# Dense output products regrouped at the head of each fox and rwkv step, and the next tile's rows turned later

## The reference, cut to what matters

```
h = rms_norm(x, norm_g);  proj = h @ w_in                       # five groups of columns
ya = spatial_gating(...)                                        # 128-token chunks
yb = forgetting_attention(q, k, v, f, q_g, k_g)                 # "fox": causal softmax over all earlier tokens
yc = mlstm(...);  ym = memory_attention(...)
yd = rwkv7_time_mix(r, w_lo, k, v, a_lo, ...)                   # recurrence over tokens, 4 heads of 64
mixed = concat([y * silu(z) for y, z in branches])              # 2048 x 1280
x = x + mixed @ w_out                                           # 1280 x 1024
```

## Time and profile before

| | |
|---|---|
| median of 3 runs | 5005.95 us (4989.76 to 5011.58) |
| profiled execution | 5015.02 us, its span 5013.4 us |
| mean granted TensorE clock | 0.857 of full speed |
| PE busy | 4250.0 us, 85% of the span |
| DVE / ACT / POOL busy | 2656.4 / 1937.1 / 732.9 us |
| steps k = 2 to 15 of the fox and rwkv loop | 1380.2 to 2489.1 us |

### The profile page before, as it was taken

One profiled execution on the slowest core, in us unless ns is written; L12 is line 12 of the kernel. 1 busy time (PEld: TensorE's weight loads), 2 busy tenths in 40 slices (PEclk: granted clock), 3 DMA queues, 4 the chain that ended last, 5 costly groups with the idle time before them and its releaser, 6 DMA issues. The chain is left out here.

```text
span 5013.4 us, 66174 instructions
## 1 busy us (share of the span) xinstructions
PE 4250.0 (85%) x23522; PEld 3149.5 (63%) x23522; DVE 2656.4 (53%) x5590; ACT 1937.1 (39%) x4022; POOL 732.9 (15%) x755
## 2 busy tenths in 40 slices
PE   7997899985788899989879999977788887877589
PEld 5885777775566666666658888833344444555467
DVE  3113444444566655555411111068889888888546
ACT  3112232323333333333311101034677767767621
POOL 3111111100100000000000000022223333434500
PEclk9998999986588888989889999966578887787789
DMA  5326656664465555454352211210000001010033
GB/s 187 123 108 218 221 201 226 199 214 148 143 215 198 194 172 177 158 173 154 113 183 90 82 66 69 59 60 19 19 20 20 20 20 38 20 39 18 32 136 116
DMA packets 293737, 585.32 MB, mean 117 GB/s; under 512 B 47944, under 2 KB 80364, under 8 KB 293244
## 3 DMA queue, kind: packets, MB, share of 16 engines
q1 hardware_dynamic: 293408, 581.10, 34.1%
HBM read 453.03 MB, written 127.94 MB: 116 GB/s over the span
## 5 line engine op out<-in xcount | busy, mean ns | idle before, releaser
L3051 PE MATMUL ds_big<-ds_ikT,ds_iqT 64*128 64x512 f32 (+3 forms) x608 | 385.2, 767 | 76.3 <-ACT ds_iqT L3028 56.4
L3518 POOL TENSOR_TENSOR ds_E<-ds_bT 128x256 f32<-128x256 f32 x112 | 72.1, 643 | 2410.9 <-ACT ds_bT L3487 2232.1
L301 PE MATMUL g_acc<-g_ws_hi,g_hT_hi 128*128 128x512 f32 (+1 forms) x1024 | 386.9, 378 | 0.0
L302 PE MATMUL g_acc<-g_ws_lo,g_hT_hi 128*128 128x512 f32 (+1 forms) x1024 | 385.3, 376 | 0.0
L303 PE MATMUL g_acc<-g_ws_hi,g_hT_lo 128*128 128x512 f32 (+1 forms) x1024 | 385.2, 376 | 0.0
L529 PE MATMUL mm_big<-mm_gw_hi,mm_ghT_hi 128*128 128x512 f32 (+1 forms) x768 | 322.0, 419 | 30.9 <-PEq L134 30.9
L3107 DVE TENSOR_SCALAR_CACHE_REDUCE ds_seen<-ds_eq,ds_num 128x2048 uint16<-128x2048 uint16 (+13 forms) x224 | 331.3, 1479 | 26.3 <-issue 4.3
L531 PE MATMUL mm_big<-mm_gw_hi,mm_ghT_lo 128*128 128x512 f32 (+1 forms) x768 | 303.2, 395 | 0.0
L530 PE MATMUL mm_big<-mm_gw_lo,mm_ghT_hi 128*128 128x512 f32 (+1 forms) x768 | 302.7, 394 | 0.0
L3147 ACT ACTIVATE ds_signs<-ds_lo,ds_at 128x2048 bf16<-128x2048 uint16 (+13 forms) x224 | 291.3, 1301 | 2.1 <-issue 0.7
L328 DVE COPY g_stage<-g_acc 128x512 f32<-128x512 f32 (+1 forms) x64 | 41.5, 649 | 459.2 <-PE g_acc L303 459.2
(11 more groups left out here) (550 smaller groups left out, 10117.7 us busy)
## 6 DMA issues: line engine op xcount, KB each, us to landing
fox_ow<-halves SPq DMA_DIRECT2D x600, 256.0 KB, 3.2
mm_ghT_hi<-turned SPq DMA_DIRECT2D x96, 512.0 KB, 4.0
mm_ghT_lo<-turned SPq DMA_DIRECT2D x96, 512.0 KB, 5.1
proj<-g_stage SPq DMA_DIRECT2D x112, 256.0 KB, 2.0
proj<-mm_gstage SPq DMA_DIRECT2D x80, 256.0 KB, 5.0
mm_x<-proj SPq DMA_DIRECT2D x64, 256.0 KB, 3.7
second_raw<-in_w_in SPq DMA_DIRECT2D x56, 256.0 KB, 4.0
proj<-fp_stage SPq DMA_DIRECT2D x48, 256.0 KB, 2.0
```

What stands on the lines that cost most here:

```text
L301: pe.matmul(sums, hT.hi[:, k, tile], wt.hi[:, k, 0:width], start=(k == 0), stop=False)
L302: pe.matmul(sums, hT.hi[:, k, tile], wt.lo[:, k, 0:width], start=False, stop=False)
L3051: pe.matmul(big[:, n % 2, 0:wd], iqT[o, h // 2], b.ikT[o, x:x + wd], start=True, stop=True)\
```

## The change

The groups of `out_turn` move to 0.90, 0.925 and 0.95. In `out_product`, for steps whose first weights are there already (k > 2), eight products come together at the head (slices j = 0 and 1 whole, and of j = 2 the two that use the high weights); the rest of the first half is spread from 0.025 to 0.425 and the second half from 0.455 to 0.875, and the third product of a slice has a place of its own. The reload of a slot now stands 0.004 behind the product that frees it. Nothing is computed otherwise, and every wait is as before.

```diff
@@ out_turn
-    at = lambda g: 0.84 + 0.045 * g
+    at = lambda g: 0.9 + 0.025 * g
@@ out_product
-    at = lambda n, j: 0.005 + 0.4 * n + 0.37 * j / OUT_K
     cols = lambda n: slice(n * 512, (n + 1) * 512)
+
+    def at(n, j, a=0):
+
+        if n == 0 and j < 3 and ahead:
+            return 0.0002 * j if (j, a) != (2, 1) else 0.025
+        if n == 0 and ahead:
+            return 0.05 + 0.375 * (j - 3 + 0.4 * a) / (OUT_K - 3)
+        return 0.005 + 0.45 * n + 0.42 * (j + 0.4 * a) / OUT_K
@@ sync
-            yield at(n, j + 0.5 * a + 0.5)
+            yield at(n, j, a) + 0.004
@@ tensor
                 pe.matmul(bank, mS.hi[:, j], whi, start=(j == 0), stop=False)
                 pe.matmul(bank, mS.lo[:, j], whi, start=False, stop=False).then_inc(s.o_used, 1)
+                yield at(n, j, 1)
                 landed(pe, q + 1)
                 pe.matmul(bank, mS.hi[:, j], wlo, start=False, stop=(j == OUT_K - 1)).then_inc(s.o_used, 1)
```

## The result

| | before | after |
|---|---|---|
| median | 5008.8 us (4989.8 to 5027.6) | 5045.6 us (5030.9 to 5067.7) |
| ratio | 1 | 1.0081, 95% interval 1.0057 to 1.0105 |
| profiled execution | 5015.0 us | 5043.3 us |
| steps 2 to 15 in it | 1108.9 us | 1164.5 us |

A forecast was written before the change was run, and what follows sets the result against it. It took steps to be bound by PE's work, the clock it runs at, and an end where PE waits. End +14 and +2, clock at the end +9, clock at the head -24 gave +1 us: 5007 us, range 4985 to 5030 (overall 4962 to 5045).

The forecast's parts named there:

- clock at the head: At step starts, the slow clock ends 7.5 us earlier, at 0.25 us per us over 13 steps: 24 us gained.
- Their price, 0.25 us per us: At step heads, time taken to be saved per us less at half clock, averaged over the whole stretch.
- The end's work: From the fifth level's last PE group to the next step: 10.7 us instead of 8.2, plus 2.5 us.
- the net, 1.3: Step end's 2.5 us less 0.4 for a moved product and 0.8 for filled gaps; 14 us in 11 steps.
- Clock at the end: At step ends, the longer wait lets the clock fall earlier: 0.8 us per folded step, 9 us lost.
- SP: Loads issued by SP at the step's end and head stay hidden, gx with next to no margin; no cost.
- rival C: At step ends, a late gx load makes each of 11 steps 1 to 2 us later: +17, 5023; chance 0.06.
- A: Head pays little, end costs as worked out: +25, with one or two new slow stretches +32, 5038; chance 0.22.
- B: Head pays in full, 44 to 55 us, less 25 for the end: -20 to -30, 4980; chance 0.27.
- the price 0.36: Us saved per us less at half speed, read from steps 4 and 5 of the kernel before.
- the sign that the prediction had named against B: PE's idle time in the 10 us behind the head grows while the clock is up; no growth would favour B.

The follow-up runs named there:

- e2: The changed kernel with turns back at 0.84, 0.885, 0.93 and products within the old span, leaving the dense head alone; ratio 1.0033 to the kernel before.
- e5: Dense head with turns as before and the rest of the first half closer behind it, from 0.05 to 0.31; ratio 0.9998 to the kernel before.
- e1: The kernel before with only the turns moved, to 0.90, 0.925 and 0.95; ratio 1.0041, +20 us.
- e6: The changed kernel with the loads of the next tile's rows at 0.30 of the step instead of 0.04; ratio 1.0056 to the kernel before.
- e11: The kernel before with turns at 0.893, 0.919, 0.945, the first low part ahead of DVE's scaling; ratio 0.9976.
- e7: The changed kernel with turns at 0.893, 0.919, 0.945, the first low part ahead of DVE's scaling; ratio 1.0081 to the kernel before.

## Why the prediction was wrong

It forecast 5007 us, its range ended at 5045, and the median is 5045.6. It gave "slower" 0.26.

*The step that failed* is the last sentence of the term "clock at the head": that a second slow stretch is left "at nothing". The reason against the 24 us of gain was named there, with steps 4 and 12 as its evidence, and then given no number. The clock did rise early, in 13 of 13 steps (8 of 10 were forecast), and 96 us of half clock went. But 102 us came back 11 to 15 us into the step. The sum should have taken the products as moved: five more at the head are five fewer behind it, 76 where 149 had started between 11 and 23 us into the steps. e2 puts the term at +16 us where the sum had -24, and e5, with the products closer behind the head, has no cost left that can be told. All seven kernels with the dense head have 78 us and more of second stretches, all seven without it 38 us or less.

*Its other numbers.* The slow heads of before were taken as 13.9 us per step, 180.8 / 13; this holds the second stretches and 3.4 us at full clock, and the heads alone are 153.5 / 13 = 11.8. That 7.5 us less per head were forecast and 7.4 came (96.3 / 13) is therefore luck. The value of before was 2.1 us too high, and two heads of ten were to stay slow and none did; the two errors cancel. Their price, 0.25 us per us, was never reached, since the time at half clock came back elsewhere.

*The end's work* was worked out right. Zero to the next step 10.7 was forecast, 11.3 came in step 9; from the last DVE copy of the levels to the next step the mean of steps 4 to 14 grew by 2.9 us against 2.5 in the chain. DVE's low part queued behind the scaling, PE idle 1.70 us before the second turns: both as told. What was too small was the net, 1.3: the gaps ahead of the end were to give back 0.8 us, and PE's idle time from 30 us into the step to that copy is 2.9 us in the mean of the same steps, 3.0 before. The turns also wait 1.04 us for the second half's add.

*Clock at the end*: 9 us forecast; the half-clock time outside heads and second stretches grew by 37 us in the profile, 18 us at 0.5 and 11 at the rate of e1 (13.2 us of busy time for 44.7 us). With e1 the end as a whole costs 20 us, with the stretching up to about 30, where the sum had 14 + 2 + 9 = 25. So this half of the forecast holds in size, and the miss of 36 us is, about, the head's 40.

*SP*: the gx load went out at 1986.84 in step 9, 8.5 us ahead of the end, and the step's last work was DVE's: rival C is out. The reload of slot 0 was hidden as told. Not seen was that the rows' three loads stand ahead of the second reloads and hold up one slice behind the head: 12.3 us more of waits, which e6 takes away again. The 29.3 us of waits that the prediction reads from the earlier trace rows count the weight loads' row (PEld) too; of matmuls waiting they are 10.0 us, the figure used here.

*Rivals.* A comes nearest: the head pays little and the end costs, +25, with new slow stretches +32 and 5038. Its stretches were two in all, at 3.6 us; there were ten more, and they cost as much as the heads won. Its test, "the clock rises less than about 4 us earlier", was the wrong one: it rose 7.4 us earlier in the mean, and the kernel was slower. B rested on the price 0.36 of the earlier trace rows, which is a price for half-clock time in the whole step and not in the head. With it the test should have been set on the sum of a step. Step 14 of the changed kernel, just after its clock rose:

```profile
2358.40:2368.00 9.60, 8.03 (x35) 4.86 (x33) 8.75 (x22) 1.88 (x6) 0.00 (x0) 1.00 0.93 300
```

8.03 us busy of 9.60, before 8.00 of 9.60, so this step alone shows no difference. Over the 13 steps PE's idle time in the 9.6 us behind the rise went from 11.7 to 22.2 us: the four steps that had 17.7 us and more of slow head had next to none of it before. That is the sign that the prediction had named against B.

*The rise of the clock.* The Trainium skill, "TensorE: Matmul & The Clock Gate", Part 1, has activity release a throttled clock; the heads of the changed kernel agree (5.10 of 5.10 us busy, then full clock), the slow heads before (17.80 of 17.80 us busy at half clock) and step 15 of e2 (33.20 of 33.20) do not. I used it for the rise alone. Whether the clock stays up is another question, and the trace shows a fall in 12 of 13 steps after the dense run was over.

*What stays open*: what makes the clock fall behind the dense head, since idle times as long did not bring it down before the change and closer products did not keep it up in e5; why the same head left the clock at half for 33.2 us in step 15 of e2; why the fix of the end moves the median by 33 us without the other parts (e1 to e11) and not with them (after to e7); and how much of the second stretches is due to weights that land late.

## What to carry to other kernels

Work that is gathered in one place is taken from another: before pricing the dense run, look at what PE has left in the 20 us behind it, and sum the half-clock time over the whole step. When an instruction is moved to a later place, read on each engine what it now stands behind; here 0.007 of a step in the place of the turns was worth 33 us by the ratios of e1 and e11, since DVE's low part went from ahead of a waiting instruction to behind it. With the rest of the change in place the same edit moved nothing that can be told (e7), so such a gain has to be measured again in the kernel that it is meant for. Look also at loads that nobody waits for and that stand ahead of reloads that somebody does: in e6 moving them took 12 us of waits away, though no gain in time is shown.

## What the runs showed of the hardware

- In the changed kernel eight 128x128 by 128x512 products in a row, then the logits, brought the granted clock from half to full 3.1 to 5.1 us after the step's start in all 13 steps, while mixes of small products with a PE row as full (17.80 of 17.80 us) had stayed at half for 17.8 us. It is no rule: in the seven kernels with this head the clock rose within 6 us in 83 of 91 heads. The others took 9.3 to 33.2 us, the longest in step 15 of e2 with PE busy throughout.
- The full clock was lost again in 12 of 13 steps of the changed kernel 11 to 15 us into the step, with no idle time of PE over 1.8 us between rise and fall. In step 14 PE was busy 8.03 of the 9.60 us behind the rise; before the change it was busy 8.00 of 9.60 there, and the clock stayed.
- The half-clock time of 13 steps stayed between 196 and 295 us in all 14 kernels, however it was spread between heads, second stretches and ends. In the changed kernel and in e2 the heads were cut and the second stretches grew by more.
- Half-clock time had no fixed price: per us more of it PE was busy 0.47 us longer in the changed kernel (19.9 for 42.7) and 0.30 in e1 (13.2 for 44.7).
